# Attention of a two-layer hybrid block: the order of weighted values and maxima on TensorE

## What is computed

```
q, k = rmsnorm(q), rmsnorm(k), rotated             # 8 query heads, 2 key heads of 64
k_all = latent keys (1024) + cached keys (128)      # 9 tiles of 128 keys
s = q . k / sqrt(64)
p = exp(s - max over the keys of s) ; o = (p @ v) / sum of p
```

## Time and profile before

| what | us |
|---|---|
| median of 3 runs (1845.34, 1849.5, 1848.46) | 1848.46 |
| the profiled execution, its own time | 1844.25 |
| its span, first to last instruction | 1842.6 |
| attention of layer 1, from S(0) to the last gate product | 575.27 to about 808.4 |
| attention of layer 2 | 1493.77 to about 1726.9 |

### The profile page before, as it was taken

One profiled execution on the slowest core, in us unless ns is written; L12 is line 12 of the kernel. 1 busy time (PEld: TensorE's weight loads), 2 busy tenths in 40 slices (PEclk: granted clock), 3 DMA queues, 4 the chain that ended last, 5 costly groups with the idle time before them and its releaser, 6 DMA issues. The chain is left out here.

```text
span 1842.6 us, 40839 instructions
## 1 busy us (share of the span) xinstructions
PE 1678.3 (91%) x17404; PEld 1367.6 (74%) x17404; DVE 978.3 (53%) x1476; ACT 623.5 (34%) x1238; POOL 928.4 (50%) x858
## 2 busy tenths in 40 slices
PE   4999999989988899979849999999899888999798
PEld 3898999979975445548728989999799754455586
DVE  2646316377736785552126563164677467955611
ACT  4322310144443444451133223111444424444511
POOL 1003395089943878832210033950899448788332
PEclk8999999999988999989969999999999999999899
DMA  9301113110000020032283011121100000200222
GB/s 338 120 14 59 61 58 93 59 37 21 4 11 13 6 58 17 12 115 92 82 308 124 31 59 61 58 85 64 39 22 4 12 13 6 64 12 12 115 91 92
DMA packets 71247, 117.22 MB, mean 64 GB/s; under 512 B 10129, under 2 KB 42129, under 8 KB 71057
## 3 DMA queue, kind: packets, MB, share of 16 engines
q1 hardware_dynamic: 70128, 114.18, 18.3%
q10 hardware_dynamic: 928, 0.34, 0.1%
HBM read 95.03 MB, written 19.47 MB: 62 GB/s over the span
## 5 line engine op out<-in xcount | busy, mean ns | idle before, releaser
L1426 POOL TENSOR_TENSOR attn_accp<-attn_accp,attn_pr 128x1024 f32<-128x1024 f32 x112 | 268.7, 2399 | 49.3 <-ACT attn_pr L1492 43.3
L93 PE MATMUL ps<-h_hi,in_w_hi 128*128 128x384 f32 (+1 forms) x816 | 275.9, 338 | 5.0 <-DVE h_lo L456 4.9
L94 PE MATMUL ps<-h_lo,in_w_hi 128*128 128x384 f32 (+1 forms) x816 | 274.6, 336 | 0.0
L95 PE MATMUL ps<-h_hi,in_w_lo 128*128 128x384 f32 (+1 forms) x816 | 274.4, 336 | 0.0
L1679 DVE TENSOR_REDUCE attn_ql<-ps 128x1 f32<-128x1152 f32 x128 | 172.9, 1356 | 119.9 <-PE ps L1606 119.5
L1492 ACT ACTIVATE attn_pr<-ps 128x512 f32<-128x512 f32 x292 | 158.6, 595 | 189.9 <-PE ps L1643 189.1
L93 PEld LDWEIGHTS ps<-h_hi,in_w_hi 128*128 128x128 f32 (+1 forms) x816 | 150.1, 184 | 13.1 <-issue 6.7
L94 PEld LDWEIGHTS ps<-h_lo,in_w_hi 128*128 128x128 f32 (+1 forms) x816 | 150.2, 184 | 3.9
L95 PEld LDWEIGHTS ps<-h_hi,in_w_lo 128*128 128x128 f32 (+1 forms) x816 | 150.1, 184 | 3.9
L1642 PEld LDWEIGHTS ps<-attn_QH,attn_KH 128*128 128x128 f32 x292 | 55.0, 188 | 126.3 <-issue 53.5
L1652 PE MATMUL ps<-attn_pr,z 128*64 128x512 f32 x520 | 141.3, 622 | 0.0
(11 more groups left out here) (248 smaller groups left out, 3604.3 us busy)
## 6 DMA issues: line engine op xcount, KB each, us to landing
in_w<-in_w_in SPq DMA_DIRECT2D x22, 1024.0 KB, 6.0
zz<-in_w_mod SPq DMA_DIRECT2D x8, 2048.0 KB, 13.3
gates<-in_gate SPq DMA_DIRECT2D x48, 192.0 KB, 1.9
attn_gt<-gates SPq DMA_DIRECT2D x34, 256.0 KB, 2.6
z<-in_w_mod SPq DMA_DIRECT2D x4, 2048.0 KB, 10.2
out_w<-in_w_out SPq DMA_DIRECT2D x16, 512.0 KB, 7.0
delta_GB<-gc_rows SPq DMA_DIRECT2D x36, 128.0 KB, 2.9
z<-out_y SPq DMA_DIRECT2D x9, 512.0 KB, 10.7
```

What stands on the lines that cost most here:

```text
L93: nc.tensor.matmul(out, a_hi(i), b_hi(i), start=(i == 0), stop=False)
L94: nc.tensor.matmul(out, a_hi(i), b_lo(i), start=False, stop=False)
L95: last = nc.tensor.matmul(out, a_lo(i), b_hi(i), start=False, stop=(i == n - 1))
L1426: nc.gpsimd.tensor_tensor(acc, a, pr[:, n % 4], ALU.add).then_inc(pool_added, 1)
```

## The change

In PE's program alone, the order within the slots changes. In an even slot V(n) is left out; in the odd slot after it V(n-1) and V(n) are issued one behind the other. In an odd slot the maximum, which stood right behind S(n+1), now stands behind these two; the turns and the sum of an odd slot stay ahead of them. The last step (72) keeps its own V. No instruction is added or removed, and the programs of ACT, DVE, POOL and SP are as they were.

```diff
         for n, items in enumerate(slots):
             if n + 1 < len(ATTN_STEPS):
                 scores(n + 1)
+            second = n % 2 == 1 and n < len(ATTN_STEPS)
             for item in items:
-                work(item)
-            if n < len(ATTN_STEPS):
+                if not (second and item[0] == "max"):
+                    work(item)
+            if second:
+                weighted_values(n - 1)
+                weighted_values(n)
+                for item in items:
+                    if item[0] == "max":
+                        work(item)
+            elif n == len(ATTN_STEPS) - 1:
                 weighted_values(n)
```

## The result

The changed kernel takes 1879.97 us (median of 4 runs, 1877.49 to 1881.7); the kernel before, in the same comparison, 1846.9 (4 runs). Ratio 1.0176, 95% interval 1.016 to 1.0193. Run again in a second comparison: 1877.25 (6 runs) against 1850.3 (17 runs), ratio 1.0154, interval 1.0129 to 1.0178. It is slower, by 33 us in the one and 27 in the other. The forecast was 1875 in 1862 to 1887.

The account below looks back on a forecast made before the run. PE's issue order was taken to bound the plain attention slots; terms summed to 14.6 less 1.4, 13.2 us per layer, +26.4 on the 1848.5 median, so 1875 us, range 1862 to 1887.

Parts of the forecast that it names:

- The wait of M' for R: Even slot's maximum (M') waits for the reduction (R) of the odd slot's maximum: PE stands 0.78 us, 24 pairs per layer.
- Merging's gain of 0.35: Odd slots: issuing two V's together saves 0.35 us, from V spacing, one narrow-form entry and one exposed weight load.
- the entry into the narrow form: At M to V, the change to narrow matmuls costs 0.09 us; merging saves one entry per odd slot.
- The rule that the prediction took from the Trainium skill: Weight loads overlap running matmuls only with different row groups; by it merging's 0.35 us would be 0.
- The "lo" waits: Slots 26, 44, 62: S waits for the turn's copy; PE stands 0.85 us, plus 0.10 exposed load, three per layer.
- The tail: From step 65 on, POOL's last additions hide slower pairs on PE, costing nothing; the layer's end moves with S(65) alone.
- Slots 0 to 8: Start of the attention: three pairs' growth enters an existing wait, but V(6) and POOL's later chain cost 1.3 us.
- the pause for POOL: Before the "hi" turn of slot 7, PE already waits 1.44 us for POOL; 1.5 us of growth goes into it.
- My rival of the falling clock: PE's clock falls in the new pauses: one V per pair at low level, 43 us more, 1918 us; chance 0.03.
- Slots 22 to 30: DVE-bound stretch: only the first maximum's later start remains, +1.0 us instead of 2.4, taking 1.4 off the layer sum.
- A count: Turns in even slots used to hide V's entry: 0.09 us x 15, 1.3 us per layer.
- The sum: Terms total 14.6 us per layer, less 1.4 beside other work: 13.2, or +26.4 us for both layers.

Follow-up runs that it names:

- chosen_slots: Kernel before, with V(n-1) merged with V(n) only in slots 9, 12, 14, 16, 25, 34, 43, 52, maxima unmoved: 1849.1 us against 1850.3, ratio 0.9994.
- merge_only: Changed kernel, but the odd slots' maxima stay right behind the scores while values are still merged: 1864.3 us, ratio 1.008 to the kernel before.
- behind_only: Changed kernel without merging: each slot issues its own values, odd slots' maxima stand behind them: 1886.0 us, ratio 1.0205 to the kernel before.

## Why the prediction was right

The direction, the mechanism and the size held. By stretches of layer 1, between maxima of even slots (starts from the timelines; the forecast's share from its own terms):

| stretch | before | after | difference | forecast |
|---|---|---|---|---|
| S(0) to M of slot 8 | 33.03 | 37.59 | +4.6 (+2.6 in the second profile) | 1.3 |
| to M of slot 22 | 48.07 | 51.01 | +2.9 | about 3.5 |
| to M of slot 30 | 26.55 | 25.49 | -1.1 | +1.0 |
| to M of slot 60 | 87.93 | 95.22 | +7.3 | about 7.4 |
| to S(65) | 8.51 | 8.89 | +0.4 | about 0.4 |
| S(65) to the last gate product | 28.99 | 28.98 | 0.0 | 0 |

- *The wait of M' for R.* 0.78 forecast, 0.77 measured; M to M' 2.35 forecast, 2.33 to 2.42 measured over the 24 pairs of layer 1, 2.33 or 2.34 in fifteen of them. Two sets of banks take it away, and the loss with it.
- *Merging's gain of 0.35.* Measured as 0.35 per merging where nothing else changes (chosen_slots), and by the difference of 3.1 over slots 32 to 59 with two sets. So the exposed weight load and the entry into the narrow form are real costs. The rule that the prediction took from the Trainium skill, "TensorE: Matmul & The Clock Gate", section "The mechanism", that a weight load overlaps running matmuls only where the row groups differ, doesn't hold in this trace: a load of S stands at 643.44 to 643.63, inside the matmul record that starts at 643.33 and lasts 0.50 (slot 18 before), and both use rows 0 to 64.
- *The "lo" waits.* 0.85 forecast; slot 26 shows the turn's first matmul at 673.53, the copy's end at 674.76, the scores at 674.81, so 0.05 behind the copy and not 0.15: 0.75 of pause. Three per layer, as forecast. The latency for which I took DVE's 0.15 is shorter behind ACT.
- *The tail.* Unchanged from S(65) on, as forecast: POOL's additions hide pairs that are slower on PE.
- *Slots 0 to 8, a term that was mis-sized*: 1.3 forecast, 4.6 and 2.6 measured. The prediction reckoned the values at the high clock and only the pause for POOL. But of the two maxima in slot 0 the second waits 1.6 us, behind which PE is at 1.2 GHz (granted clock 0.50). Before, V(0) and part of the S behind it stood at that clock; in the changed kernel it is all of slot 1, S, sum and two V's:

```profile
580.44:587.44 7.00, 7.00 (x21) 2.88 (x21) 1.36 (x1) 1.79 (x3) 2.35 (x1) 0.61 0.00 0
584.04 2.83 PE L1652 MATMUL ps<-attn_pr,z 128*64 128x512 f32 x8
```

  The eight records take 2.83 where they take 1.94 at the high clock. With two sets of banks, where that pause is gone, the slot takes 4.40 at clock 1.00. In slot 7 the clock fell in one profile of two, 1.5 us. My rival of the falling clock was priced for the plain slots, where it didn't happen; it happened here.
- *Slots 22 to 30, mis-sized the other way*: +1.0 forecast, -1.1 measured. I held DVE's work fixed and added the later start. The gate products of slots 22 to 29 took 12.7 us together before (8 of them) and 10.5 after (9), and slots 27 and 28 alone became 1.6 shorter: their gate products took 2.55 and 2.45 before, both beside an addition of POOL, and 2.55 and 0.68 after. I read this as another phase against POOL's additions. No run isolates it, and the stretch moves with the order: 29.07 in merge_only, 25.91 in behind_only. This and the step above nearly cancel in the sum (13.2 forecast, 14.1 and 12.7 measured up to S(65)); that part of the agreement is luck.
- *A count.* Of the even slots up to 62, 18 hold a turn, where the forecast counted 15; at 0.09 each that is 0.3 per layer, and with it the last column of the table adds up to 13.6 and not 13.2.
- *The sum.* Attention of both layers: +26.4 forecast, +28.3 and +25.6 measured in the two profiles. The profiled executions of the first comparison differ by 33.2, of which some 5 lie in the other stages.

## What to carry to other kernels

Before two like operations are grouped, look at what used to lie between the neighbours that they now push together: a producer with one PSUM buffer needs its consumer's whole round (here 2.33 us from one maximum to the next) filled with other work, and the grouping's gain of 0.35 was paid with a wait of 0.77. Read the distances between starts in the trace and compare them with that round; where a distance has slack, the order is free, and where it has none, either a second buffer or nothing. Take the round with what the consumer does besides: in slot 9 it was 4.32 us and not 2.33, because the reduction stood behind another piece of work. For differences of a few microseconds, compare the stretch between two instructions that both kernels have, since the stages that weren't touched moved by 12 us between profiles.

## What the runs showed of the hardware

- The clock behind a pause isn't the same from run to run. In one program, with the same 1.58 us pause and the same instructions, slot 7 ran at a granted clock of 0.76 once and 1.00 once. The last "sum" of a layer, behind 2.9 to 3.4 us of idle PE, took 1.08 us in ten of the eighteen layers profiled and 1.36 to 1.98 in the other eight; it ran at 1.00 in the kernel before and at 0.50 in chosen_slots. In the plain slots, with a pause of 0.77 in every 5.9 us, it stayed at 1.00.
- Two V's of eight records take 0.43 from one group of matmuls to the next inside the run, but 0.48 after the entry, and the first weight load of the wide form behind them costs 0.10: M's record is 0.79 behind V, 0.69 behind S.
